# Splitting the last expert's down weights in another place, and loading the next stage's rows before a pass of experts ends

## What is computed

```
in_grp = e_logits of the token's one group           # top-1 of 4 groups
top_p, top_local = top_k(softmax(in_grp), 2)         # top-2 of its 8 experts
y_e = (silu(xb @ w_gate[e]) * (xb @ w_up[e])) @ w_down[e]
y[token] += y_e[slot] * gate[slot]                   # two slots a token
h = h + y
```

## Time and profile before

| what | value |
|---|---|
| median of three runs | 2118.39 us |
| the profiled execution's own time | 2113.19 us |
| its span, first to last instruction | 2111.5 us |
| mean granted TensorE clock | 0.919 of full speed |
| data moved by DMA | 374.40 MB, 177 GB/s on average |
| ScalarE and VectorE, share of the span | 41% and 58% |

### The profile page before, as it was taken

How to read it: one execution, slowest core, us unless ns; L and a number is a source line. 1 busy time by engine, 2 the same in 40 slices (tenths; PEclk the granted TensorE clock), 3 DMA queues, 4 the chain that set the end, 5 groups by cost and what they waited for, 6 DMA issues and landing times. The chain is left out here.

```text
span 2111.5 us, 25605 instructions
## 1 busy us (share of the span) xinstructions
PE 1817.7 (86%) x9608; PEld 1505.6 (71%) x9608; DVE 1223.1 (58%) x1566; ACT 865.3 (41%) x928; POOL 316.9 (15%) x258
## 2 busy tenths in 40 slices
PE   8999998376898999949999982999999949999980
PEld 7888887364677788837888761888887847888760
DVE  5323333755645445558999866332325557999973
ACT  4102222312333342227888863211102127888860
POOL 0000000101000001122434310000000122343410
PEclk9999999867899999969999995999999969999995
DMA  5333332602000024277999948211206258999947
GB/s 204 130 116 125 102 126 86 135 1 80 1 1 1 1 82 157 90 292 273 376 378 370 373 191 289 78 40 50 68 32 218 100 232 317 380 383 372 377 160 309
DMA packets 145297, 374.40 MB, mean 177 GB/s; under 512 B 40078, under 2 KB 75150, under 8 KB 120446
## 3 DMA queue, kind: packets, MB, share of 16 engines
q1 hardware_dynamic: 113542, 309.54, 39.9%
q0 software_dynamic: 22432, 45.53, 6.0%
q10 hardware_dynamic: 9216, 17.93, 2.2%
HBM read 331.38 MB, written 75.10 MB: 193 GB/s over the span
## 5 line engine op out<-in xcount | busy, mean ns | idle before, releaser
L1253 PE MATMUL ex_ps_h<-odd_split 128*128 128x512 f32 x768 | 196.1, 406 | 8.1 <-DVE odd_split L1367 7.9
L1253 PE MATMUL ex_ps_h<-even_split 128*128 128x512 f32 x768 | 195.1, 405 | 8.3 <-DVE even_split L1367 8.0
L1253 PEld LDWEIGHTS ex_ps_h<-odd_split 128*128 128x128 f32 x768 | 142.4, 192 | 47.5 <-DVE odd_split L1367 14.4
L1253 PEld LDWEIGHTS ex_ps_h<-even_split 128*128 128x128 f32 x768 | 142.0, 191 | 47.4 <-DVE even_split L1367 14.3
L517 PE MATMUL in_ps<-in_w_hi,in_xT_hi 128*128 128x512 f32 (+1 forms) x448 | 172.1, 384 | 1.7 <-DVE in_xT_lo L422 1.7
L517 PE MATMUL in_ps<-in_w_lo,in_xT_hi 128*128 128x512 f32 (+1 forms) x448 | 169.0, 377 | 0.0
L517 PE MATMUL in_ps<-in_w_hi,in_xT_lo 128*128 128x512 f32 (+1 forms) x448 | 168.9, 377 | 0.0
L1640 PE MATMUL conv_ps<-conv_xT_hi,conv_w_hi 128*128 128x512 f32 x384 | 150.5, 392 | 0.9 <-DVE conv_w_lo L1578 0.9
L1640 PE MATMUL conv_ps<-conv_xT_lo,conv_w_hi 128*128 128x512 f32 x384 | 149.9, 390 | 0.0
L1640 PE MATMUL conv_ps<-conv_xT_hi,conv_w_lo 128*128 128x512 f32 x384 | 149.9, 390 | 0.0
L2349 ACT ACTIVATE att_prob<-att_ps_s 128x512 f32<-128x512 f32 x114 | 68.0, 597 | 175.0 <-PE att_ps_s L2287 174.8
(11 more groups left out here) (343 smaller groups left out, 3981.4 us busy)
## 6 DMA issues: line engine op xcount, KB each, us to landing
all_region<-in_moe_w_gate SPq DMA_DIRECT2D x16, 1024.0 KB
all_region<-in_moe_w_up SPq DMA_DIRECT2D x16, 1024.0 KB
all_region<-in_moe_w_down SPq DMA_DIRECT2D x16, 1024.0 KB
experts_w_gu<-in_moe_w_gate SPq DMA_DIRECT2D x16, 1024.0 KB
experts_w_gu<-in_moe_w_up SPq DMA_DIRECT2D x16, 1024.0 KB
experts_w_d<-in_moe_w_down SPq DMA_DIRECT2D x16, 1024.0 KB, 15.6
all_region<-in_ev_w_in SPq DMA_DIRECT2D x12, 1024.0 KB, 8.2
proj<-in_stage ACTq DMA_DIRECT2D x48, 256.0 KB, 2.1
```

Source lines behind the costliest of these rows:

```text
L1253: last = pe.matmul(ps_h[:, u % 2, :], a[:, u % 2, k, :], w[:, k, :], start=(k == 0 and j == 0), stop=(k == KT - 1 and j == 2))
```

## The change

1. In the last step ScalarE and VectorE split the down weights of expert 31 not in DOWN's place but in the place of FIRST (`last_down`), which is free once TensorE has done FIRST of expert 31. The split moves ahead of the silu on ScalarE (`high_last`) and ahead of the product on VectorE (`low_last`); TensorE's last `down` reads the new place.
2. SyncE loads the next stage's rows as soon as expert 28 has been split (tiles 0 to 5) and the token rows of experts 28 and 29 have been turned (tiles 6 and 7), instead of after VectorE's last instruction. Where further waves run, the rows are loaded once more behind them.
3. GpSimd reads the fullest expert's count into its register at the start of the block instead of behind its last scatter; SyncE reads it behind the loads of point 2.

```
@@ class Split
+    def last_down(self):
+        return [self.part(j * KT * 2 * DE, DE // P, D) for j in range(2)]
@@ class NextRows
-    def load(self, sp):
-        for t in range(NT):
-            sp.dma_start(self.rows[:, t, :], self.src[t * P:(t + 1) * P, :]).then_inc(self.loaded[t], 16)
+    def load(self, sp, tiles):
+        for t in tiles:
+            sp.dma_start(self.rows[:, t, :], self.src[t * P:(t + 1) * P, :]).then_inc(self.loaded[t], 16)
+
+    def load_again(self, sp, loaded):
+        for t in range(NT):
+            sp.dma_start(self.rows[:, t, :], self.src[t * P:(t + 1) * P, :]).then_inc(loaded, 16)
@@ experts
+        last_down = data.split.last_down()
...
-        done, finished = m.sb("done", [P, 1]), m.sem("finished")
+        done, finished, reloaded = m.sb("done", [P, 1]), m.sem("finished"), m.sem("reloaded")
...
-        def waves(eng, body, first=0):
-            if first == 0:
-                body(0)
-            full = eng.value_load(most[0:1, 0:1], min_val=0, max_val=CAP)
+        def fullest(eng):
+            return eng.value_load(most[0:1, 0:1], min_val=0, max_val=CAP)
+
+        def later_waves(eng, full, body, begin=None, end=None):
             with eng.If(full > P):
+                if begin:
+                    begin()
                 with eng.Fori(1, CAP // P) as w:
                     with eng.If(full > w * P):
                         body(w)
+                if end:
+                    end()
...
-            waves(eng, wave)
+            wave(0)
+            later_waves(eng, fullest(eng), wave)
@@ sync
-                waves(sp, wave, first=1)
-
-                sp.wait_ge(finished, 1)
-                following.load(sp)
+                for piece in (SECOND, DOWN):
+                    sp.wait_ge(piece_lo[piece], NE - B + 1)
+                following.load(sp, range(NT - 2))
+                for e in range(2):
+                    sp.wait_ge(x_turned[e], NE // B)
+                following.load(sp, range(NT - 2, NT))
+
+                def landed():
+                    for t in range(NT):
+                        sp.wait_ge(following.loaded[t], 16)
+
+                def load_again():
+                    sp.wait_ge(finished, 1)
+                    following.load_again(sp, reloaded)
+                    sp.wait_ge(reloaded, 16 * NT)
+                later_waves(sp, fullest(sp), wave, landed, load_again)
@@ gpsimd
+                full = fullest(pool)
...
-                waves(pool, wave, first=1)
+
+                def landed():
+                    for t in range(NT - 2, NT):
+                        pool.wait_ge(following.loaded[t], 16)
+                later_waves(pool, full, wave, landed)
@@ tensor
-                def down(n, u):
+                def down(n, u, hi=d_hi, lo=d_lo):
...
-                            for j, (a, w) in enumerate(((h_hi, d_hi), (h_hi, d_lo), (h_lo, d_hi))):
+                            for j, (a, w) in enumerate(((h_hi, hi), (h_hi, lo), (h_lo, hi))):
...
-                    down(*last)
+                    down(*last, *last_down)
@@ scalar
+                def high_last(n, u):
+                    act.wait_ge(down_loaded[u % B], 16 * uses(n, u) + 16)
+                    act.wait_ge(piece_used[FIRST], n * U + (u + 1))
+                    act.activation(last_down[0], data.raw(DOWN, u % B), ACT.Copy).then_inc(piece_hi[DOWN], 1)
...
                     if not isinstance(n, int):
+                        act.wait_ge(piece_used[DOWN], n * U)
...
                     hidden(*last)
                     if following:
                         high(*following, FIRST)
+                    else:
+                        high_last(*this)
                     gate(*this)
                     if following:
                         tokens(*following)
                         high(*following, SECOND)
                     rows_out(*last)
-                    high(*this, DOWN)
+                    if following:
+                        high(*this, DOWN)
@@ vector
+                def low_last(n, u):
+                    dve.wait_ge(piece_hi[DOWN], n * U + (u + 1))
+                    hi, lo = last_down
+                    dve.tensor_tensor(lo, data.raw(DOWN, u % B), hi.bitcast(F32), ALU.subtract).then_inc(piece_lo[DOWN], 1)
...
                     hidden(*last)
                     if following:
                         low(*following, FIRST)
+                    else:
+                        low_last(*this)
                     product(*this)
                     if following:
                         tokens(*following)
                         low(*following, SECOND)
-                    low(*this, DOWN)
+                        low(*this, DOWN)
```

## The result

The changed kernel takes 2095.43 us (median of 4 runs, 2092.64 to 2096.34), the kernel before 2118.95 beside it; the ratio is 0.9892 with a 95% interval of 0.9874 to 0.9909. The forecast was 2095.6. The four runs of the kernel before include the three that the forecast started from. The profiled execution took 2095.42 us, its span 2093.8.

A forecast was written before the change was run, and what follows sets the result against it. TensorE bounds on average, but a single thread of waits bounds the passes' ends. Split, clock, rows and count save 11.15 us (odd) and 11.6 (even), 22.8 together: 2095.6 us by ratio; likeliest range 2090 to 2101, whole 2088 to 2106.

The forecast's parts named there:

- The split: Wait before each pass's last down: early split of expert 31's down weights starts that down 3.7 us earlier per pass.
- The clock: Last down at full clock: 2.55 us (odd), 2.4 (even) saved; rival, clock falls all the same, 2099.6, chance 0.15.
- The rows: Ends of both passes: last scatter lands alone in 3.2 us, saving 4.2 us (odd) and 4.7 (even).
- a landing over 4 us: Sign in the profile after: last scatter taking over 4 us to land, not 3.2, would make the forecast wrong by that amount.
- the cover: Rival: next stage's rows still moving when the last scatter comes; gain 13.9 us, time 2104.5, chance 0.06.
- The count: GpSimd's register load between last scatter's landing and branch leaves the thread: 0.7 us (odd), 0.8 (even).
- The sum: Ends of both passes together: 11.15 us (odd) and 11.6 (even), 22.8 in all, giving 2095.6 us.
- a late split: Rival: expert 31's weights come too late for the early split, TensorE waits as before; gain 10.5 us, 2107.9, chance 0.02.
- The slower case: Rival: rows served ahead of expert 31's gates, which land up to 13 us later; time about 2132, chance 0.04.
- the shared case: Rival: DMA engines shared half and half, expert 31's gates delayed about 6 us; time as before, 2118, chance 0.03.

The follow-up runs named there:

- the halves: Changed kernel with GpSimd's branch ahead of the scatter waits, plus ScalarE copying the last two results out in halves: 2087.65 us, ratio 0.9867 to the kernel before.
- the rows alone: Kernel before with only the next stage's rows loaded early, the down split in its old place and the count read late: 2107.98 us, ratio 0.9964.
- the count alone: Kernel before with only GpSimd's read of the fullest expert's count moved to the block's start: 2114.49 us in a single run.
- second profile: Changed kernel run again unaltered, beside two further kernels on the same chip: median 2094.11 us, ratio 0.9900 to the kernel before.

## Why the prediction was right

*The split.* Right to 0.05 us: idle 1.63 where 1.6 was forecast, bound by ScalarE's copy of expert 30's result, as the halves confirm, which shorten just that.

*The clock.* Right in outcome, 2.3 and 2.45 of 2.4 and 2.55. These are the sizes of one profile: the same down behind the same 5.35 us idle took 4.7 to 5.2 us in the kernels with the rows alone and the count alone, so in other executions the term is 1.8 to 2.2. The 0.63 that the prediction read as the last down's clock isn't that: 8 of those 13 us lie behind the down, whose own clock was 0.50 from 2055.3 to 2060.8. The term came from durations, so the sum doesn't suffer. The reason given, that a gap up to 1.85 us had kept the clock, was safe but not sharp; gaps to 2.2 kept it here. All four last downs of the two profiles of the changed kernel ran at full clock.

*The rows.* Right in mechanism; the size of the landing was off. It was taken as 3.2 us, the one lone scatter of the profile before. In the changed kernel the last ones took 4.1 and 3.6, in its second profile 4.7 and 3.7. That is the mis-sized term: 0.9 and 0.4 us of the 1.5 by which 22.8 is more than 21.3; the clock's 0.1 a pass is the rest. The prediction called a landing over 4 us a sign of being wrong, and the even pass shows it in both profiles. The rows are long done by then, and all that moves while the last scatter is under way is 62 and 61 GB/s, the scatter included, so it isn't the cover. What makes a lone scatter land in 3.2 or in 4.7 was not found.

*The count.* 1.5 us forecast; gone from the queue as said (landing 2053.0, branch 2053.1). Alone it brought 1.15.

*The sum.* 22.8 was 1.5 too much by the profile. The forecast time was already moved to the median of the runs before, and the medians then differed by 23.5, more than the ends give, within an interval of 19 to 27. That the time came out within 0.2 us of the forecast is luck; what the stretches bear out is 21.3.

*The rivals.* Neither the clock, the cover nor a late split came. The slower case was priced from the whole 4 MB being served first, a delay of 13 us, and the shared case at some 6. With the rows on a queue of their own the odd pass's down weights came 2.6 us later, and the time didn't suffer, so the shared case was priced too high. That the rows are served first altogether was not brought about by any run.

What the prediction did not say is that the split and the rows lean on each other: without the early rows the split keeps 9.3 of its 12.2 us, since the earlier scatter falls deeper into the transfers (landing 8.5 us instead of 8.0 and 7.5) and the branch behind it comes upon their tail (3.1 and 3.3 us instead of 2.6).

## What to carry to other kernels

At a pass's end, follow the thread of single waits to the next stage's first transfer: there each term counts in full, and the last step can use the places that a missing successor leaves free. Load what the next stage wants when its place comes free, not when the pass ends; then the last store lands alone. Behind the pass's last loads in their own queue it doesn't delay them; on another queue it did by 2.6 us, at no cost that the time shows here. Take a branch, and whatever is fetched for it, before the wait that ends a block, not behind it.

## What the runs showed of the hardware

- GpSimd's branch to the block's end cost 2.6 to 2.9 us before its next instruction in the profiles without transfers beside it, and 3.1 and 3.3 with the tail of the rows' transfers (111 and 76 GB/s). In between one packet of a DMA queue of the kind `instruction` moved. The Trainium skill ("Runtime: NRT & Kernel Launch", Instruction fetch mechanics) tells of such a stall for a branch whose target has to be fetched by DMA; the trace agrees, by that packet, and the number is this case's.
- A scatter beside the rows' 4 MB (338 GB/s from 2056 to 2069 in the kernel before) landed in 7.4 to 8.5 us, alone in 3.2 to 4.7.
- TensorE kept 2.4 GHz over idle times of 1.63, 2.02 and 2.22 us and lost it for a part of the next matmuls after 2.62 and 2.81, and in the attention of the kernel before after 2.04.
